# Attention beside the input projection, and its norm and two output units inside the state space head loop

## The reference, cut to what matters

```python
mod = silu(c) @ w_ada + b_ada                       # 6 x 2048 modulation values
h = rms_norm(x, g) * (1 + scale_m) + shift_m
q, k, v, xs, z, bmat, cmat, dt_raw = split(h @ w_in)
attn = rms_norm(attention(q, k, v, rel_bias), attn_norm_g)      # 8 heads of 128, causal
ssm = ssd_mixer(xs, z, bmat, cmat, dt_raw, ...)     # 16 heads of 64, conv of 4 taps, own norm in 2 groups
x = x + gate_m * (concat([attn, ssm]) @ w_out)
h = rms_norm(x, g2) * (1 + scale_f) + shift_f
x = x + gate_f * conv_ffn(h, ...)
```

## Time and profile before

| | |
|---|---|
| median of 3 runs | 2530.37 us (2530.3 to 2535.34) |
| the profiled execution's own time | 2534.03 us |
| its span | 2532.3 us |
| PE busy | 2407.7 us, 95% of the span |
| DVE busy | 1915.2 us, 76% |
| ACT busy | 1153.8 us, 46% |
| bytes moved | 614.70 MB, 243 GB/s over the span |

### The profile page before, as it was taken

One profiled execution on the slowest core, in us unless ns is written; L12 is line 12 of the kernel. 1 busy time (PEld: TensorE's weight loads), 2 busy tenths in 40 slices (PEclk: granted clock), 3 DMA queues, 4 the chain that ended last, 5 costly groups with the idle time before them and its releaser, 6 DMA issues.

```text
span 2532.3 us, 42221 instructions
## 1 busy us (share of the span) xinstructions
PE 2407.7 (95%) x17090; PEld 2143.6 (85%) x17090; DVE 1915.2 (76%) x2294; ACT 1153.8 (46%) x1290; POOL 87.8 (3%) x184
## 2 busy tenths in 40 slices
PE   8999969899999999999899899999999999999997
PEld 6899848788888888888799788889888888888887
DVE  6778878888787888888988666668888664566655
ACT  2144373355554345554444345533565543455442
POOL 0010000000000000000000000000000000000000
PEclk9999979999999999999999999889999999999999
DMA  9998837677777887778588123218577555555552
GB/s 399 421 336 334 342 141 307 258 283 287 273 291 292 344 318 277 273 265 328 216 309 300 56 89 111 101 52 316 228 276 259 184 194 186 184 188 190 185 217 100
DMA packets 88530, 614.70 MB, mean 243 GB/s; under 512 B 9657, under 2 KB 13393, under 8 KB 15057
## 3 DMA queue, kind: packets, MB, share of 16 engines
q1 hardware_dynamic: 65218, 444.03, 46.8%
q0 software_dynamic: 23184, 168.83, 17.6%
HBM read 608.60 MB, written 4.22 MB: 242 GB/s over the span
## 4 chain that ended last, share of the span: by engine, by line
PE 73%; DVE 12%; DMA 8%; ACT 4%; issue 2%; DVEq 0%; POOLq 0%; SPq 0%; ACTq 0%
PE ps L770 37%; PE ps L772 19%; DMA ada_raw<-in_ada_stream 4%; PE ps L765 3%; PE ps L766 3%; PE ps L767 3%; DMA first_raw<-in_ada_stream 2%; DVE ada_raw L1705 2%; DVE w_lo L1693 1%; DMA w_raw<-in_w_stream 1%; PE ps L762 1%; DVE first_raw L1705 1%; ACT w_hi L1157 1%; PE ps L651 1%; DVE w_lo L1689 1%
## 5 line engine op out<-in xcount | busy, mean ns | idle before, releaser
L770 PE MATMUL ps<-h_both,w_hi 128*128 128x512 f32 x2816 | 995.4, 399 | 15.2 <-DVE h_both L1736 14.4
L772 PE MATMUL ps<-h_both,w_lo 128*128 128x256 f32 x2816 | 790.2, 281 | 0.0
L770 PEld LDWEIGHTS ps<-h_both,w_hi 128*128 128x128 f32 x2816 | 531.4, 189 | 146.7 <-issue 16.5
L1689 DVE TENSOR_TENSOR w_lo<-w_raw,w_hi 128x2048 fp32r<-128x2048 f32 x217 | 495.6, 2288 | 97.9 <-ACT w_hi L1151 90.9
L772 PEld LDWEIGHTS ps<-h_both,w_lo 128*128 128x128 f32 x2816 | 533.7, 190 | 0.0
L1151 ACT CAST w_hi<-w_raw 128x2048 fp32r<-128x2048 f32 x218 | 415.3, 1911 | 251.9 <-DMA w_raw<-in_w_stream 235.4
L770 PE MATMUL ps<-hid_both,w_hi 128*128 128x512 f32 x1344 | 466.4, 390 | 1.6 <-DVE w_lo L1693 1.6
L765 PE MATMUL ps<-h_both,w_hi 128*128 128x256 f32 x1408 | 409.6, 291 | 27.8 <-DVE h_both L1736 14.9
L1693 DVE TENSOR_TENSOR w_lo<-w_raw,w_hi 128x2048 fp32r<-128x2048 f32 x139 | 318.0, 2289 | 132.4 <-ACT w_hi L1157 132.3
L766 PE MATMUL ps<-h_both,w_hi 128*128 128x256 f32 x1408 | 401.8, 285 | 0.0
L767 PE MATMUL ps<-h_both,w_lo 128*128 128x256 f32 x1408 | 401.5, 285 | 0.0
(11 more groups left out here) (363 smaller groups left out, 2055.5 us busy)
## 6 DMA issues: line engine op xcount, KB each, us to landing
w_raw<-in_w_stream SPq DMA_DIRECT2D x364, 1024.0 KB, 4.9
ada_raw<-in_ada_stream POOLq DMA_DIRECT2D x160, 1024.0 KB, 7.0
first_raw<-in_ada_stream SPq DMA_DIRECT2D x32, 1024.0 KB, 12.6
w_more<-in_w_stream SPq DMA_DIRECT2D x8, 1024.0 KB, 14.7
kept_raw<-in_w_stream SPq DMA_DIRECT2D x4, 1024.0 KB, 8.3
x<-in_x_t SPq DMA_DIRECT2D x1, 2048.0 KB, 7.9
cs_b<-cs_rows SPq DMA_DIRECT2D x4, 512.0 KB, 6.8
x_kept<-x SPq DMA_DIRECT2D x1, 2048.0 KB, 13.9
```

Of the source, the lines that this page charges most:

```text
L770: mm(ps[:, b, :].rearrange("p (a t) -> p a t", a=2), hi, both[:, :, k], start=first, stop=False, skip_group_check=True)
L772: return mm(ps[:, b, T:512], lo, big[:, k], start=False, stop=False, skip_group_check=True)
L1689: tt(w_lo[:, slot], w_raw[:, slot], w_hi[:, slot].bitcast(F32), ALU.subtract).then_inc(lo_ready, 1)
```

## The change

Attention is taken out of its place between the head loop and the output projection. Its scores, transposes and products with v now stand between the units of the input projection, first the heads 0 to 3, then 4 to 7; z and v change places in the stream, so that v is there in chunks 4 and 5. To make room in PSUM, the chunks of the input projection take two banks with two tiles in each (`tile_of`, `paired`), which leaves banks 4 to 7 to attention. Attention's norm is applied inside the head loop, by `att_scaled` and `att_lower` on DVE and `att_upper` on ACT, and from head 8 on PE does a quarter of an output unit behind each head (`out1_piece`), two units in all. The four pairs of `HEAD_ADA` and three of the four that stood in attention move: one pair stays behind the gating, and 23 instead of 16 now stand in the output projection (`out1_ada`). As `logit` and `cs_b` now lie in the memory of `x`, SP loads `x` (2 MB) again behind the head loop.

```diff
-HEAD_ADA = (2, 6, 10, 14)
...
+            units(KT, KT + 2)
+            sp.wait_ge(bias_out, 16)
+            sp.wait_ge(n_t, N_H1 + KT)
+            sp.wait_ge(ada_done, ADA_FIRST)
+            for b in range(2):
+                src = bass.AP(tensor=scratch, offset=b * 4 * 384, ap=[[1, P], [384, 4], [1, T]])
+                sp.dma_start(bias[b][:], src).then_inc(bias_in[b], 16)
+            units(KT + 2, U_IN1 + 25)
             sp.wait_ge(S("decays"), 1)
             sp.dma_start(cs_rows.ap(), dtcs[:, 1, :]).then_inc(S("cs_out"), 16)
+            units(U_IN1 + 25, U_OUT1)
             sp.wait_ge(S("cs_out"), 16)
-            units(U_OUT1, U_OUT1 + 3)
-
-            sp.wait_ge(units_used, U_OUT1 + 2)
+            sp.wait_ge(S("pv"), 2)
...
+            units(U_OUT1, U_OUT1 + 4)
+            sp.wait_ge(S("decay_diff"), SSM_HEADS)
+            sp.dma_start(x[:], a["x_t"]).then_inc(x_in, 16)
...
+            def out1_piece(i, j):
+                pe.wait_ge(lo_ready, U_OUT1 + i + 1)
+                pe.wait_ge(n_lo, N_ATT + 4 * i + 4)
+                w_h, w_l = w_hi[:, slot_of(i, U_OUT1)], w_lo[:, slot_of(i, U_OUT1)]
+                for kk in range(4):
+                    k, w = 4 * i + kk, slice(kk * 512 + j * P, kk * 512 + j * P + P)
+                    last = three(bank(j), w_h[:, w], w_l[:, w], h_hi[:, k], h_lo[:, k], k == 0, False)
...
+            scores(0)
+            in1(1)
+            in1(2)
+            in1(3, 0, 1)
+            pe.wait_ge(con_in, 48)
+            turn_probs(0)
+            in1(3, 1, 4)
+            pe.wait_ge(S("prob_t"), 1)
+            scores(1)
+            in1(4)
+            in1(5)
+            in1(6, 0, 1)
+            turn_probs(1)
+            in1(6, 1, 3)
+            pe.wait_ge(S("prob_t"), 2)
+            opens(IN1 + 7)
+            attend(0)
+            in1(6, 3, 4)
+            in1(7, 0, 1)
+            pe.wait_ge(S("att_out"), 1)
+            attend(1)
+            in1(7, 1, 3)
...
+            stat(1, b=7)
+            in1(7, 3, 4)
...
             for h in range(SSM_HEADS):
                 ssm_head(pe, mm, h)
+                if h == 8:
+                    opens(OUT1 + 1)
+                if h >= 8:
+                    out1_piece((h - 8) // 4, h % 4)
...
+                if h == 1:
+                    in1_evac(7, 1)
+                    hi(0, 1, U_OUT1)
+                if 2 <= h < 10:
+                    att_upper(h - 2)
...
-            SOFTPLUS = {(5, 3): 0, (6, 0): 1, (6, 3): 2}
+            SOFTPLUS = {(3, 3): 0, (4, 3): 1, (5, 2): 2}
...
+                    if (c, i) in ((1, 1), (4, 1)):
+                        logits(c // 3)
+                    if (c, i) in ((2, 1), (5, 1)):
+                        inverse_sums(c // 3)
...
                 if h >= 2:
                     head_y(h - 2)
-                if h in HEAD_ADA:
-                    next_ada()
+                if h == 2:
+                    lo(0, 1, U_OUT1)
+                if h < 8:
+                    att_scaled(h)
+                if 3 <= h < 11:
+                    att_lower(h - 3)
...
-            stream(U_OUT1, OUT1, 0, 4, add_to_x(U_OUT1, GATE_M), 64, 4)
+            out1_ada = ((0, 0, 2, 2), (1, 2, 1, 2), (1, 2, 1, 2), (2, 2, 1, 2))
+            for c in range(4):
+                for i in range(4):
+                    if c:
+                        lo(c, i, U_OUT1)
+                    if c and i == 1:
+                        if c == 1:
+                            dve.wait_ge(x_in, 32)
+                        add_to_x(U_OUT1, GATE_M)[0](c - 1, (OUT1 + c - 1) % 2)
+                    next_ada(out1_ada[c][i])
```

More of the change, by code:

```diff
@@ L193, in build_program @@
             pool_raw = sb(under, "pool_raw", [P, HT, T])
+        with ExitStack() as under:
+            cs_b = sb(under, "cs_b", [P, SSM_HEADS, T])
+        with ExitStack() as under:
+            logit = [sb(under, f"logit{b}", [P, 4, 384]) for b in range(2)]
+            bias_a = sb(under, "bias_a", [P, 4, T])
         x = sb(ctx, "x", [P, KT, T])
@@ L248, in build_program @@
             qk = sb(s, "qk", [P, 16, T])
+            with ExitStack() as under:
+                x_tok = sb(under, "x_tok", [P, 2, WIDTH])
             v_tok = sb(s, "v_tok", [P, 2, WIDTH])
@@ L252, in build_program @@
             relb = sb(s, "relb", [HEADS, BUCKETS])
[L253 to L259, removed]
+            bias, prob_t = [bias_a, bias_b], logit
+            att_m = [sb(s, f"att_m{b}", [P, 8]) for b in range(2)]
+            att_s = [sb(s, f"att_s{b}", [P, 8]) for b in range(2)]
+            att_r = [sb(s, f"att_r{b}", [P, 8]) for b in range(2)]
             with ExitStack() as t:
@@ L462, in _ @@
                 sp.dma_start(cs_b[:, 4 * q:4 * q + 4], src).then_inc(side_loaded[q], 16)
[L463 to L474, removed]
+            units(U_OUT1, U_OUT1 + 4)
+            sp.wait_ge(S("decay_diff"), SSM_HEADS)
+            sp.dma_start(x[:], a["x_t"]).then_inc(x_in, 16)
             def load_kept(name, k):
                 src = a["w_stream"][U_KEPT[name] + k]
[L477 removed]
+                sp.dma_start(kept_raw[:, k], src).then_inc(S(f"kept_in{k}"), 16)
             units(U_OUT1 + 4, U_DN1B + 8)
@@ new lines, in turn_probs, with attend @@
+            def turn_probs(b):
+                pe.wait_ge(S("scores_read"), b + 1)
+                pe.wait_ge(S("probs"), b + 1)
+                for i in range(4):
+                    for j, src in enumerate((256, 0, 128)):
+                        last = nc.tensor.transpose(ps[:, 4 + i, j * P:j * P + P], logit[b][:, i, src:src + P], ident[:])
+                last.then_inc(S("probs_turned"), 1)
+            def attend(b):
+                for i in range(4):
+                    h = 4 * b + i
+                    mm(ps[:, 4 + i, 0:T], v_tok[:, 0, h * P:h * P + P], prob_t[b][:, i, 0:T], start=True, stop=False)
+                    last = mm(ps[:, 4 + i, P:T], v_tok[:, 1, h * P:h * P + P], prob_t[b][:, i, T:384], start=False, stop=True)
+                last.then_inc(S("pv"), 1)
@@ L1243, in in1_evac @@
                         j = 4 * (c - 1) + i
-                        last = A(xbc[:, j], bank(4 * par_ + i), ACT.Identity, bias=pcol("ssm_cb", j),
+                        last = A(xbc[:, j], tile_of(par_, i), ACT.Identity, bias=pcol("ssm_cb", j),
                                  scale=pcol("ssm_cw", 4 * j + 3))
@@ L1270, in _ @@
                     A(sp_w[:, 4, 0:1], pcol("a_log", rows=16), ACT.Exp).then_inc(S("dt_exp"), 1)
+                if c == 6:
+                    attended(0)
+            attended(1)
+            act.wait_ge(S("att_out"), 2)
+            stat(1, [qk[:, k] for k in range(HT)], N_H1 + 16)
             hi(0, 0, U_OUT1)
-            in1_evac(7, 1)
-            hi(0, 1, U_OUT1)
+            root(1)
             def decay_diff(h):
@@ L1285, in decay_diff, with att_upper @@
                 last.then_inc(S("decay_diff"), 1)
+            def att_upper(k):
+                act.wait_ge(n_t, N_ATT + k + 1)
+                A(h_hi[:, k], tmp[:, (N_ATT + k) % 4], ACT.Identity, bias=pcol("zero")).then_inc(n_hi, 1)
             act.wait_ge(S("dt_tok"), 1)
```

309 lines of the change are left out of this document (146 added, 163 removed).

## The result

The changed kernel takes 2557.76 us in the median of 4 runs (2556.51 to 2559.37), the kernel before beside it 2532.86 us (4 runs, 2530.3 to 2538.84). The ratio is 1.0095, with a 95% interval of 1.0077 to 1.0113: slower by 25 us. The forecast was 2554 us.

What follows compares the result with a forecast made beforehand. PE bounds the kernel, DVE close behind; 23 pairs in two slots would hold up the output projection, ending it 23.5 us later. 2534.0 plus 23.5 gives 2557.5, median 3.7 lower: 2554 us, 8-in-10 range 2528 to 2572.

Steps and rivals of the forecast that it cites:

- The input projection: Stage that receives attention: 17.2 us more PE work, 3.5 small products and 5 of stalls, turned x at 335.5 us.
- The head loop: Sixteen heads after the turned x, the last eight bound by PE: 33 us, last head at 368.5.
- Behind the loop: Gating, pair and norm work between last head and output projection: 16.3 us, PE resuming at 384.8 instead of 389.6.
- The pairs: Output projection, 23 pairs in two slots: period 10.3 us, 9 for the first two, 111 us, last pair ending at 501.
- the upper end: Slow end for the slot period in the output projection: 11.0 us as now, last pair at 509, 31 us late.
- Behind the last pair: End of the output projection: a `w_lo`, the reduction of 5.6 us and the last addition, 23.5 us later than before.
- The second load of x: 2 MB in the pause behind the head loop, needed 25 us later: costs nothing, or 5 us of bus time if late.
- The rest of the kernel: From the feed forward part on: order the same as before, no change in time counted.
- The signs: Expected in the trace: gap 50 us or less, PE well under 90% busy, DVE waiting over 25 us, pairs every 5 us.
- The rival of hidden loads: Output projection: loads land in the 5.1 us of the pause, period 8.0, 2519 us in all; chance 0.13.
- The second rival, the memory's own rate: Output projection: period 8.3 to 8.6 us set by memory, no change, 2528 to 2535 us; chance 0.13.
- The third rival: Input projection falls behind as well, PE waiting for `probs` and `prob_t`: 10 to 15 us added, about 2567; chance 0.16.

Runs made afterwards that it cites:

- experiment 5: Two kernels, each the changed kernel with one edit: first output unit loaded ahead of the decays' broadcasts, 2556.91 us; first input projection pair loads held back, 2552.18 us.
- Experiment 1: The kernel before with only the modulation pairs moved (the pairs alone), 23 instead of 16 in the output projection, attention left in place: 2552.89 us, ratio 1.0055.
- experiments 3 and 4: Changed kernel with four places for pairs: 2540.17 us (four in flight), 2542.15 (three), 2560.34 (two); changed kernel with eight pairs moved out of the output projection: 2533.36.
- all edits: Changed kernel with pairs spread anew, four places for pairs 65 to 76, output unit loaded before the decays, first pair loads held back: 2526.34 us, ratio 0.9953.
- section 6: Kernel with all edits, 2526.34 us; the same without output units in the head loop, 2526.9; the same with 19 pairs in the output projection, 2530.95.

## Why the prediction was right, and where its sizes were off

The time, 2557.76 against 2554, is as forecast, and so is the mechanism of the output projection. That the time is so close is in part luck: PE resumes the output projection 6.5 us later than the sum had it, and 1.7 us from the periods and 3.6 from the rest of the kernel, where nothing was changed, take most of that back. By its own steps:

- *The input projection.* The turned x was put at 335.5 us; its transposes run from 335.13 to 337.04. The stage began 2 us late, which was not in the sum (the wait of 3.1 us below is the one in front of it), and the stalls of 5 us were 4.8: 2.2 at 241.7 us in chunk 4, behind the convolution, the logits and a pair, as forecast, and 2.6 at 255.4, at the first unit of chunk 5, behind a pair and softplus. From the waits of PE, 140 to 339 us:

```profile
PE ps L813 <- DVE w_lo L1736: 4.8, 2, 2.6
PE ps L762 <- DVE qk L1893: 3.1, 1, 3.1
```

- *The head loop* was the worst-sized term: 33 us forecast, the last head at 368.5; it came at 375.3, 38 us after the turned x. Two things were missed. The first output unit, issued behind the decays' broadcasts, took 17.43 us to land in the chain of the changed kernel, and ScalarE's cast of it, its table changes and exponentials followed in order:

```profile
314.61 17.43 DMA w_raw<-in_w_stream
332.08 1.90 issue
333.99 1.28 ACT L1205
335.70 1.38 ACT lm L1358 x4
337.10 1.28 ACT L1372
```

  Undoing that order alone took 3 us off the loop (experiment 5). And a head with its quarter unit took 2.41 us, not 2.07: in the same chain the head at 360.34 is followed by the next at 362.76, with PE full at a clock of 1.00. In the first half, from 346 to 358 us, ScalarE was busy for 11.62 of 12 us and DVE for 11.30, PE for 8.46 at a granted clock of 0.55: there the two others set the pace. So the output projection resumed at 391.3 instead of 384.8 us, and the gain of 4.8 us that the sum had at this point was a loss of 1.7, beside the two units done.

- *Behind the loop:* 16.3 us forecast, 16.0 measured (375.3 to 391.3).
- *The pairs.* 111 us for 11 periods from the first pair's end were forecast, 109.3 measured. The estimate 10.3 a period from landing plus 2.9 was 4% too long, since loads landed in 6.8 us and not in 7.4: with PE waiting, fewer units are on the bus (13 in 115 us). Experiment 1 has the same period without attention's move, experiments 3 and 4 remove most or all of the loss by more in flight or by fewer pairs: the step is shown, not only argued. What the sum did not see is the other part of experiment 1, that the move itself would give nothing ahead of this stage. A slip in the upper end: with the first two periods at 9 us, 11.0 for the rest gives 507.4 us for the last pair, and 11.0 throughout 511.4, not 509.
- *Behind the last pair:* the reduction took 5.37 us instead of 5.62, and the last addition is 28.3 late where 23.5 was the sum; the first pair ended 6.5 us later than forecast (396.9 against 390.4), and the periods gave 1.7 of it back.
- *The second load of x* cost nothing, as taken: nothing in the waits of DVE from 391 to 507 us names it.
- *The rest of the kernel* was taken as unchanged. The span is longer by 24.7, not 28.3. The last product with `u_tok` starts at 1689.9 us before and 1718.3 after (28.4 late), the last operation of the last convolution at 2414.5 and 2439.1 (24.6). But this stretch of 724.6 and 720.8 us takes 729.4 with all edits and 727.9 with the pairs alone, kernels that are the same there. So the 4 us are not a gain of the change but what one execution differs from another; over its first 100 us the granted clock is 0.91 before (1690 to 1790 us), 0.96 after (1718 to 1818), 0.94 with the pairs alone (1715 to 1815) and 0.91 with all edits (1685 to 1785), which does not order the four as their times do.
- *The signs.* Most came: PE was busy for 77% of the output projection, DVE waited 28.2 us for pairs, a pair came every 5.0 us and one of PE's units every 8.2. Two did not. The gap was to be 50 us or less and was 53.3; and the reduction to `mix_sum` was to begin several us after PE's last unit, but began at 508.4 us, before the last matmul of that unit (509.5), as it stands directly behind that unit's `w_lo`.

The rival of hidden loads fell by the landing: 6.8 us, not under 5.5. The Trainium skill, in DMA: Bandwidth & Descriptors (Anatomy of one DMA, SWDGE path), has a fixed 2.0 us and the bytes over 436 GB/s, an estimate of 4.4 us for such a load; only the shortest load on the chain above (4.96 us) comes near it, and with four in flight the same load takes 12 to 13 us. The second rival, the memory's own rate, came near only with more loads in flight (a DMA share of 0.93 with four). The third rival, further stalls in the input projection, did not occur: the stalls were the 4.8 us of the sum, and what came late came in the head loop.

## What to carry to other kernels

When work is moved to fill a pause, ask who else used the pause: here it was where loads landed quickly and eight of 80 pairs were made. Test the two halves of such a change apart: here the new order left the next stage's end 6.9 us later than the old order with the same pairs. Before moving a stream, multiply the uses of a slot by (landing + pass + issue) and compare the product with the stage; if it is longer, another load in flight (the third gave 21 us at the mark, the fourth at most 4) or a place where the consumer idles (29 us) was worth more here than the rearrangement of the matmuls. And don't judge such a stage by how long a load takes to land, but by how many land in it.

## What the runs showed of the hardware

The landing time of a 1 MB load grows with the number in flight, and beyond three the rate hardly does: in the 80 us from 400 on, 7.2 to 7.9 us at 343 GB/s with two pair loads in flight beside the weights, 8.3 to 10.3 at 392 with three, and 9.1 to 13.4 at 396 with four. The rows of the windows for two and three in flight in that stretch:

```profile
400.00:480.00 80.00, 63.78 (x468) 62.60 (x467) 58.13 (x49) 18.32 (x10) 8.45 (x16) 0.87 0.91 343
```

```profile
400.00:480.00 80.00, 68.91 (x531) 67.95 (x530) 71.54 (x60) 24.88 (x15) 9.17 (x18) 0.94 0.97 392
```

The DMA share is not the distance from that limit: it reads 0.91 at 343 GB/s, and a third load still brought 49 GB/s more. The granted clock of TensorE rises in the same rows: 0.87 where it waits for data (63.78 of 80 us busy), 0.94 at 68.91. What a pause costs beyond itself is seen in section 6: after 10.49 us of idleness 16 matmuls took 6.69 us, after 1.55 us 3.69.
